# Norms between the stages of a three-layer transformer kernel, done in two halves of 256 tokens

## What is computed

```python
h = x
for layer in range(2):
    u = rms_norm(h, mix_norm_g[layer])
    h = h + mixer(u)                       # ends in o @ w_out, 1024 x 1024
    h = h + square(relu(rms_norm(h, mlp_norm_g[layer]) @ w_up)) @ w_down
h = rms_norm(h, final_norm_g)
a = rms_norm_2(h, norm_mix)                # of h with 16 meta tokens in front
h = h + mix(a) @ w_o
h = h + square(relu(rms_norm_2(h, norm_mlp) @ w_up)) @ w_down
return rms_norm_2(h, norm_final)
```

## Time and profile before

| | before |
|---|---|
| median of 3 runs | 2329.89 us (2322.6 to 2332.05) |
| the profiled execution | 2321.05 us |
| its span in the profile | 2319.1 us |
| PE busy | 2180.8 us, 94% |
| DVE, ACT, POOL busy | 1048.8, 759.6, 335.1 us |
| loads, mean over the span | 79 GB/s |

### The profile page before, as it was taken

How to read it: one execution, slowest core, us unless ns; L and a number is a source line. 1 busy time by engine, 2 the same in 40 slices (tenths; PEclk the granted TensorE clock), 3 DMA queues, 4 the chain that set the end, 5 groups by cost and what they waited for, 6 DMA issues and landing times.

```text
span 2319.1 us, 26170 instructions
## 1 busy us (share of the span) xinstructions
PE 2180.8 (94%) x10791; PEld 1718.3 (74%) x10795; DVE 1048.8 (45%) x1550; ACT 759.6 (33%) x1214; POOL 335.1 (14%) x308
## 2 busy tenths in 40 slices
PE   6988988999999899979999998999999999999997
PEld 5755556888888777667888886866778767888886
DVE  3659743333333457744333334255656434333333
ACT  3225552433232234433322323133433323423221
POOL 2210000211010011101100102111145320201000
PEclk9989999999999999989999998999999999999999
DMA  5330002223223221012223223221111223232231
GB/s 141 108 91 19 20 1 73 91 97 100 94 95 106 76 73 40 34 57 96 93 91 109 91 91 97 82 71 53 55 55 56 73 73 100 91 109 91 91 109 55
DMA packets 163505, 182.59 MB, mean 79 GB/s; under 512 B 19701, under 2 KB 123562, under 8 KB 163386
## 3 DMA queue, kind: packets, MB, share of 16 engines
q1 hardware_dynamic: 161066, 174.11, 23.9%
q0 software_dynamic: 2320, 6.80, 1.2%
HBM read 177.75 MB, written 2.17 MB: 78 GB/s over the span
## 4 chain that ended last, share of the span: by engine, by line
PE 87%; DVE 6%; ACT 2%; issue 2%; DMA 1%; SPq 1%; POOL 1%; ACTq 0%; POOLq 0%; DVEq 0%
PE banks L357 71%; PE banks L2315 2%; PE banks L1124 1%; PE banks L1160 1%; PE banks L1044 1%; DVE wl L335 1%; PE banks L2434 1%; ACT wh L331 1%; PE banks L397 1%; PE banks L1555 1%; PE banks L1617 1%; PE banks L2055 1%; PE banks L2084 1%; PE banks L2005 1%; PE banks L1479 1%
## 5 line engine op out<-in xcount | busy, mean ns | idle before, releaser
L357 PE MATMUL banks<-uTh,wh 128*128 128x512 f32 x1344 | 540.4, 402 | 14.3 <-DVE wl L335 4.2
L335 DVE TENSOR_TENSOR wl<-stg,wh 128x2048 fp32r<-128x2048 f32 (+1 forms) x154 | 353.6, 2297 | 413.7 <-ACT wh L331 413.3
L357 PE MATMUL banks<-wh,hTr 128*128 128x512 f32 x1696 | 527.5, 390 | 6.2 <-DVE wl L335 4.9
L357 PE MATMUL banks<-uTh,wl 128*128 128x512 f32 x1344 | 526.5, 392 | 0.0
L357 PE MATMUL banks<-uTl,wh 128*128 128x512 f32 x1344 | 526.3, 392 | 0.0
L331 ACT ACTIVATE wh<-stg 128x2048 fp32r<-128x2048 f32 (+1 forms) x154 | 292.8, 1903 | 440.9 <-PE banks L357 410.4
L357 PEld LDWEIGHTS banks<-wh,hTr 128*128 128x128 f32 x1696 | 319.2, 188 | 73.1 <-DVE wl L335 5.3
L357 PE MATMUL banks<-wl,hTr 128*128 128x512 f32 x848 | 330.4, 390 | 0.0
L357 PEld LDWEIGHTS banks<-uTh,wh 128*128 128x128 f32 x1344 | 254.8, 190 | 72.8 <-issue 14.1
L357 PEld LDWEIGHTS banks<-uTh,wl 128*128 128x128 f32 x1344 | 254.0, 189 | 54.7
L357 PEld LDWEIGHTS banks<-uTl,wh 128*128 128x128 f32 x1344 | 254.9, 190 | 52.4 <-issue 2.4
(11 more groups left out here) (350 smaller groups left out, 2262.4 us busy)
## 6 DMA issues: line engine op xcount, KB each, us to landing
stg<-mlp_w_up SPq DMA_DIRECT2D x32, 1024.0 KB, 5.3
stg<-mlp_w_down SPq DMA_DIRECT2D x32, 1024.0 KB, 5.0
stg<-w_in SPq DMA_DIRECT2D x20, 1024.0 KB, 5.2
stg<-w_up SPq DMA_DIRECT2D x16, 1024.0 KB, 5.3
stg<-w_down SPq DMA_DIRECT2D x16, 1024.0 KB, 5.0
stg<-odd_w_in SPq DMA_DIRECT2D x16, 512.0 KB, 4.8
stg<-even_cmp_w SPq DMA_DIRECT2D x4, 1024.0 KB, 5.5
stg<-odd_w_in SPq DMA_DIRECT2D x4, 1024.0 KB, 5.1
```

The costliest lines, as they stand in the source:

```text
L335: dve.tensor_tensor(lo, stage_of(k), hi.bitcast(F32), ALU.subtract).then_inc(*v_lo.next(k))
L357: t = pe.matmul(outp, x, y, start=(start and k == 0 and m == 0), stop=(stop and k == n - 1 and m == 2))
```

## The change

It touches the six norms that follow a product (n1 to n5 and the final one) and the first product after each.

- In the last half (`c` = 1) of the product in front, the order of the eight groups of 12 matmuls becomes (g, i) = 00, 01, 10, 11, 02, 03, 12, 13, so that tiles 0 and 1 are whole four groups before the end (`pe_add_norm`). Tile 0 is turned behind group 02 and tile 1 behind 03.
- DVE and ACT norm tiles 0 and 1 between their other work, and evacuate these 256 tokens (`dve_parts`, `act_parts`, phase 0), eight pieces of 256 columns each. Tiles 2 and 3 follow (phase 1).
- The next product begins on 256 tokens: `pe_first` does two groups of 8 x 3 matmuls with 256 columns on phase 0, turns tiles 2 and 3, and does the same two groups on phase 1. That is the first piece of `up`, or `nq` after n4. After n2 (`pe_values`) tokens are the weights side, and the phases only change the order.
- The turned tiles lie in other PSUM banks, the banks of the MLPs and of the values are renumbered to fit (`BANKS`), and the scaled tiles lie in the buffers P and T instead of `big`. In n4 the gained tile is written beside `h`, no longer over it, and `h` is scaled and gained at the end by four operations (L442 before).

```diff
-        def pe_add(pe, tag, lhs, nk, ready, free, banks=range(8)):
-            for c in range(2):
+        def pe_add(pe, tag, lhs, nk, ready, free, banks=range(8), cs=range(2)):
+            for c in cs:
...
+        def pe_add_norm(pe, tag, lhs, ready, free, norm, banks):
+            yield from pe_add(pe, tag, lhs, 8, ready, free, banks, (0,))
+            w = {}
+            for x, (g, i) in enumerate(((0, 0), (0, 1), (1, 0), (1, 1), (0, 2), (0, 3), (1, 2), (1, 3))):
+                if i == 0:
+                    w[g] = take(pe, tag + (1, g))
...
+                if norm in NORMS and x in (4, 5):
+                    pe_turned(pe, norm, x - 4)
+                yield
...
+        def pe_turned(pe, norm, i):
+            ph, j = divmod(i, 2)
+            pe.wait_ge(*v_norm.at((norm, "x", i)))
+            if i == 2:
+                pe.wait_ge(*v_part.at((norm, 0, KT - 1)))
+            for k in (0, 4, 1, 5, 2, 6, 3, 7):
+                t = pe.transpose(norm_rows(norm, ph, k)[:, j * 128:(j + 1) * 128], xn[i][:, k * 128:(k + 1) * 128], ident)
...
+            for g in range(2):
+                split("act", tag + (0, g))
+            for i in range(NT - 1):
+                squares(0, i)
+            split("act", tag + (1, 0))
+            squares(0, NT - 1)
+            squares(1, 0)
+            squares(1, 1)
+            split("act", tag + (1, 1))
+            if norm in NORMS:
+                act_parts(act, norm, 0)
+            squares(1, 2)
+            squares(1, 3)
+            split("act", tag + (1, 1), 2)
+            if norm in NORMS:
+                act_parts(act, norm, 1)
...
+            add(1, 0)
+            mean(0)
+            add(1, 1)
+            scaled(0)
+            mean(1)
+            scaled(1)
+            split("dve", tag + (1, 1))
+            add(1, 2)
+            if norm in NORMS:
+                dve_parts(dve, norm, 0)
+            mean(2)
+            add(1, 3)
+            scaled(2)
+            mean(3)
+            scaled(3)
+            split("dve", tag + (1, 1), 2)
+            if norm in NORMS:
+                dve_parts(dve, norm, 1)
...
+        def pe_first(pe, norm, w, banks):
+
+            for ph in range(2):
+                if ph:
+                    pe_turned(pe, norm, 2)
+                    pe_turned(pe, norm, 3)
+                for f in range(2):
+                    for k in range(KT):
+                        pe.wait_ge(*v_part.at((norm, ph, k)))
+                        t = products(pe, bank[banks[f]][:, ph * 256:ph * 256 + 256],
+                                     [(w[0][:, k, f * 128:(f + 1) * 128], w[1][:, k, f * 128:(f + 1) * 128],
+                                       *tokens(k, ph * 256, 256))], k == 0, k == KT - 1)
...
         def pe_values(pe):
...
+                for k0 in (0, 4):
+                    if ph == 0:
+                        w[k0] = take(pe, ("dv", 0, k0))
+                    for i in (2 * ph, 2 * ph + 1):
+                        for k in range(k0, k0 + 4):
+                            pe.wait_ge(*v_part.at(("n2", ph, k)))
+                        t = tm(pe, bank[DV_BANKS[0][i]], w[k0], i * 128, 128, 512, k0)
```

More of the change, by code:

```diff
@@ L426, in dve_norm_twice @@
[L426 to L442, removed]
@@ L479, in pe_add, with act_add @@
                         yield
-        def act_add(act, tag, nk, norm=None, gain=False, scratch=None):
+        def act_add(act, tag, nk):
             for c in range(2):
@@ L484, in act_add, with dve_add @@
                     split("act", tag + (c, g))
[L485 to L494, removed]
                     yield
-        def dve_add(dve, tag, nk, norm=None, gain=False, banks=range(8)):
+        def dve_add(dve, tag, nk, banks=range(8)):
             for c in range(2):
@@ L504, in dve_add @@
                         dve.tensor_tensor(hc, hc, bank[banks[c * 4 + i]], ALU.add).then_inc(*v_add.next((tag, c, i)))
[L505 to L517, removed]
-                    yield
+                    yield
+        def pe_add_norm(pe, tag, lhs, ready, free, norm, banks):
[4 more added lines that the diff above has]
+                    w[g] = take(pe, tag + (1, g))
+                if g == 0:
+                    free(pe, 1, i)
+                wh, wl = w[g]
+                t = products(pe, bank[banks[4 + i]], [(*lhs(g * 4 + k, i), wh[:, k, :], wl[:, k, :]) for k in range(4)],
+                             g == 0, g == 1)
+                names = ([(tag, 1, i)] if g else []) + ([("free", tag + (1, g))] if i == 3 else [])
+                if names:
+                    t.then_inc(*p_mm.next(*names))
+                if norm in NORMS and x in (4, 5):
+                    pe_turned(pe, norm, x - 4)
+                yield
@@ new lines, in norm_rows @@
+        def norm_rows(norm, ph, k):
+            b = bank[BANKS[NORMS[norm][0]][k % 4]]
+            return b[:, k // 4 * 256:k // 4 * 256 + 256]
+        def pe_turned(pe, norm, i):
[5 more added lines that the diff above has]
+                t = pe.transpose(norm_rows(norm, ph, k)[:, j * 128:(j + 1) * 128], xn[i][:, k * 128:(k + 1) * 128], ident)
+                if j and k >= 4:
+                    t.then_inc(*p_turn.next((norm, ph, k)))
@@ new lines, in act_parts @@
+        def act_parts(act, norm, ph):
+            _, gname, g0 = NORMS[norm]
+            s = slice(ph * 256, ph * 256 + 256)
+            for k in range(KT):
+                if k < 4:
+                    act.wait_ge(*p_turn.at((norm, ph, k + 4)))
+                else:
+                    act.wait_ge(*v_part.at((norm, ph, k - 4)))
+                act.activation(uTh[:, k, s], norm_rows(norm, ph, k), ACT.Copy, scale=col(gname, g0 + k)).then_inc(
+                    *a_part.next((norm, ph, k)))
@@ new lines, in dve_parts, with act_add_norm, squares @@
+        def dve_parts(dve, norm, ph):
+            _, gname, g0 = NORMS[norm]
+            s = slice(ph * 256, ph * 256 + 256)
+            for k in range(KT):
+                dve.wait_ge(*a_part.at((norm, ph, k)))
+                dve.scalar_tensor_tensor(out=uTl[:, k, s], in0=norm_rows(norm, ph, k), scalar=col(gname, g0 + k),
+                                         in1=uTh[:, k, s].bitcast(F32), op0=ALU.mult, op1=ALU.subtract).then_inc(
+                    *v_part.next((norm, ph, k)))
+        def act_add_norm(act, tag, norm, scratch=None):
+            gain = norm == "n4"
+            def squares(c, i):
+                act.wait_ge(*v_add.at((tag, c, i)))
+                act.wait_ge(*a_sq.now(0 if scratch else 1))
+                act.activation(scratch or Q[0 if gain else i % 2][:, 0:512], h[:, i, c * 512:(c + 1) * 512], ACT.Square,
+                               accum_out=nrm[:, i, c:c + 1]).then_inc(*a_sq.next((tag, c, i)))
+                if gain:
+                    act.wait_ge(*v_add.at((tag, c, i, "gain")))
+                    act.wait_ge(*a_sq.now(1))
+                    act.activation(Q[1][:, 0:512], xn[i][:, c * 512:(c + 1) * 512], ACT.Square,
+                                   accum_out=nrm[:, i, 2 + c:3 + c]).then_inc(*a_sq.next((tag, c, i, "gain")))
+            for g in range(2):
[14 more added lines that the diff above has]
+                act_parts(act, norm, 1)
+            yield
@@ L531, in pe_up @@
                 w = take(pe, key)
+                if q == 0 and g == 0:
+                    for f, t in enumerate(pe_first(pe, src, w, BANKS[tag])):
+                        t.then_inc(*p_mm.next((tag, "up", q, f), *([("free", key)] if f else [])))
+                    yield
+                    continue
                 for f in range(2):
@@ L597, in pe_mlp, with act_mlp, dve_mlp @@
                 yield from down(q)
-        def act_mlp(act, tag, norm, gain=False):
+        def act_mlp(act, tag, norm):
             yield from act_up(act, tag, 0)
[L601 to L606, removed]
+            for q in range(3):
+                yield from act_up(act, tag, q + 1)
+                yield from act_add(act, (tag, "down", q), 8)
+            yield from act_add_norm(act, (tag, "down", 3), norm)
+        def dve_mlp(dve, tag, norm):
             yield from dve_up(dve, tag, 0)
[L608 to L611, removed]
+            for q in range(3):
+                yield from dve_up(dve, tag, q + 1)
+                yield from dve_add(dve, (tag, "down", q), 8, BANKS[tag])
+            yield from dve_add_norm(dve, (tag, "down", 3), norm, BANKS[tag])
         def pool_mlp(pool, tag):
@@ L1339, in pe_values @@
                         if i == NT - 1:
-                            names.append(("free", key))
+                            names.append(("free", ("dv", 0, k0)))
                         if names:
                             t.then_inc(*p_mm.next(*names))
-                    yield
+                yield
+            for k0 in (0, 4):
+                key = ("dv", 1, k0)
+                w = take(pe, key)
+                for i in range(NT):
+                    t = tm(pe, bank[DV_BANKS[1][i]], w, i * 128, 128, 512, k0)
```

(18 more changed lines are left out.)

268 lines of the change are left out of this document (153 added, 115 removed).

## The result

| | before | after |
|---|---|---|
| median | 2327.26 us (4 runs, 2322.6 to 2332.05) | 2296.18 us (4 runs, 2291.98 to 2297.29) |
| profiled execution / its span | 2321.05 / 2319.1 us | 2297.29 / 2295.5 us |

The ratio is 0.9863, with a 95% interval of 0.9837 to 0.9889: 31 us faster by the medians, where 31.1 were forecast, and 2296 against a forecast of 2294. That the sum fits does not say that its terms do, so the terms follow one by one.

The account below looks back on a forecast made before the run. PE, busy 94%, was held up by 72 us of gaps at norms and the end. Gains 11.9 (n1, n3, n5) + 3.4 (n2) + 10.4 (n4) + 5.4 (end) = 31.1 us gave 2294, range 2280 to 2308.

Parts of the forecast that it names:

- What bounds the kernel: Whole kernel: PE is busy 94% of the time; the gaps at the norms and the end are together 72 us.
- So the transposes run slow there: Old norm gaps: PE's low clock puts transposes 0.18 us apart, against loads 0.11 apart at full clock.
- Prices: First products: 0.121 us per 256-column product, so 0.7 us more per first piece; eight transposes 1.2, sixteen 2.1.
- 0.29 idle at the start of such a group: Turns of a tile: 0.29 us idle added to 0.9 for eight transposes, making 1.2 us.
- n1: Plain norm, like n3 and n5: 16.7 us in place of 20.6, a gain of 3.9.
- n2: Norm n2: 8.2 us in place of 11.6, gain 3.4, with waits of 2.3 (low half) and 1.3 (four parts).
- n4: Norm n4: 20.1 us against 30.5, a gain of 10.4.
- the ledger: Each norm: step times from the last group in front; at n4 tile 2 at 6.1, tile 3 8.8, phase 1 11.5.
- the clock among the rivals: Phases 0 and 1: PE's clock falls among turns and half-wide products, costing 57 us, giving 2351; chance 0.03.
- The end: After the last matmul: 7.3 us in place of 12.7, a gain of 5.4.
- The overlap rule: Narrow products: by the skill's row-group rule load and columns would run serially, without gain; the trace disagreed for 512 and 348.

Follow-up runs that it names:

- wide_first: The change, but the next product begins only when all 512 tokens are evacuated, with 512 columns: 2319.71 us against 2324.76 for the kernel before, ratio 0.997.
- kept_busy: The kernel before, with PE given overwritten identity transposes ahead of the first turned tile: 2327.95 us against 2324.76, ratio 1.0008.
- again: The change itself, unaltered, measured once more beside later kernels: 2292.86 us against 2322.77 for the kernel before, ratio 0.9872.
- all_narrow: The change, with all other products of the up pieces done as two of 256 columns: 2322.51 us in one execution.
- split_late: The change, with DVE's half of the second piece behind the second evacuation at n1, n3, n4, n5: 2293.64 us, ratio 0.987.
- both: The change, with n2's later turns between its weight pieces and DVE's second-piece split behind the second evacuation at n1, n3, n4, n5: 2285.18 us, ratio 0.9834.

## Why the prediction was right, term by term

- **What bounds the kernel**: right. PE's idle time at the norms was the cost, and it went where PE got other work. wide_first keeps all but that work and loses nearly all of the gain, about a quarter of it to the clock behind the waits.
- **"So the transposes run slow there"**: wrong as a cost. They ran slow, but DVE's and POOL's 1.48 us a tile was the pace; kept_busy raised the clock and gained nothing. The low clock costs something where it lasts into the products, as in wide_first. The sum did not suffer, since it took the measured gap of before and the turns of after at full clock.
- **Prices**: 0.121 for a narrow product measured 0.120. The turn was charged too much: the "0.29 idle at the start of such a group" is idle time of the weight loads, and beside it PE was still busy with the products in front. In the change eight turns cost 0.87 on the chain, not 1.2, and sixteen 1.75, not 2.1. That is 1.0 a norm. At n1 the gain was 4.9 and not 3.9: from the last product in front to the end of the first piece 395.96 to 416.84 before, and 402.52 to 416.68 after, plus 1.8 for the two turns inside. Of this the stretch keeps less, since the unchanged products ahead of n1 took 1.0 more after, at 0.85 of the clock in their first 19 us against 0.90.
- **n2**: both waits came, 1.5 us (forecast 2.3) and 1.7 (1.3). The first is shorter since PE itself began 0.3 late and ran 24 products at a slightly slower pace.
- **n4**: each point within 0.3 us of the ledger, but the profiled execution lost some 2 us more in phase 1 at the low clock: 8.28 us, against 6.07 in "again". I had put the clock among the rivals with 0.03 for both phases of all norms; it came at one norm only, in some executions, behind idle time that the ledger itself had shown. The forecast put this term at nothing.
- **The end**: 5.6 for 5.4.
- **The overlap rule**: the Trainium skill ("TensorE: Matmul & The Clock Gate", Part 3, The mechanism) would serialise the load with the product, if the row group is all that counts; the same section also names the background weight buffer as a way for a load to be pulled ahead. In all_narrow products stood 0.12 apart with PE and PEld both busy for the whole 40 us, and each load is recorded with 0.19 us, as in the earlier trace rows; one after the other the two have no room there. So for full-array products of 256 columns the trace disagrees with the rule on the row group taken alone.

The errors, +1.0 at each of five norms and about -2 at n4, are smaller than the 8 us by which the unchanged rest differs between profiles. That the total came out within 2 us was partly luck.

## What to carry to other kernels

Where a row-wise norm stands between two products, doing some rows early is worth little until the next product can start on them: the work on the first half must last as long as the chain of the last tile, its evacuation included. Lay the chain out as a ledger with each engine's list in order, because what comes late next is then read off it; here it was a weight split and four evacuations, and the turns placed between two pieces covered both for 3 us more. And before counting a clock that fell in a gap as a cost, look at who sets the pace there, and at the first products behind it: in before DVE and POOL set the pace, and at four of five norms the low clock ended with the gap; in wide_first it lasted some ten products longer and cost about 2 us a norm.

## What the runs showed of the hardware

- In one and the same program, with the same 1.8 and 1.5 us of idle at n4, the clock was granted at 0.60 behind it in one execution and at 1.00 in another. What the idle costs differs from run to run, about 2 us here. In split_late, with 1.84 and 0.43 us of idle, phase 1 was granted 0.78, and in "both", with the same idle, 1.00. Nothing here tells what decides it.
- Behind a wait the low clock can last into the products: in wide_first 0.50 over the first 4.0 to 5.7 us behind n1, n3, n4 and n5, with PE busy all the time; in before 1.00 at three of these places and 0.87 at n4.
- In kept_busy PE was busy for 17 of the 20 us ahead of 1425, but its added transposes ended at n4's first turned tile. Between the turns PE then waited 1.57 us twice, the last groups of turns fell in the second window here, n4's first product began at 1430.31, and the clock stood at 0.50:

```profile
1405.00:1425.00 20.00, 17.02 (x121) 15.14 (x119) 9.58 (x28) 5.79 (x16) 3.31 (x6) 1.00 0.16 53
1425.00:1431.00 6.00, 4.63 (x18) 3.76 (x19) 3.28 (x8) 2.31 (x5) 1.72 (x4) 0.50 0.00 0
```

  So cover of PE ahead of the turns did not carry the clock across the waits between them.
- Repetitions of an unchanged stretch of 340 us differ by 8 us with the mean granted clock: 337.25 us at 0.95, 345.29 at 0.92.
